# A two-block sequence model on one core: second FFN halves tile by tile, weight low parts on VectorE, folded transforms, two decay levels put by ScalarE

## The chip, the cores and the metric

The kernel runs on one core of one Trainium2 chip. The metric is the time of one execution on the device in microseconds (us), lower is better. TensorE (PE in the rows, PEld for its weight loads), VectorE (DVE), ScalarE (ACT), GpSimd (POOL) and the DMA queues of SyncE (SP) run side by side and meet at semaphores.

## The reference, cut to what matters

Two model blocks run one after the other on 512 tokens of width 1024 and on 256 context tokens; all arithmetic is float32.

```python
def half_ffn(h, shift, scale, gate, wg, wu, wd):
    return h + 0.5 * gate * swiglu(modulate(rms_norm(h), shift, scale), wg, wu, wd)
def swiglu(x, wg, wu, wd):
    return (jax.nn.silu(x @ wg) * (x @ wu)) @ wd
def step(s, inp):                       # hgrn2_chunk_scan; the GLA of block two has the same form
    ...
    scores = jnp.einsum('bhtsd,bhsd->bhts', qb[:, :, :, None, :] * decay, kb)
    o = scores @ vb + (qb * jnp.exp(cum)) @ s
    s_new = jnp.exp(last[:, :, 0, :])[..., None] * s + jnp.einsum('bhsd,bhse->bhde', kb * jnp.exp(last - cum), vb)
def fft_conv(u, kern):
    l = u.shape[1]
    uf = jnp.fft.rfft(u.astype(jnp.float32), n=2 * l, axis=1)
    kf = jnp.fft.rfft(kern, n=2 * l, axis=0)
    return jnp.fft.irfft(uf * kf[None], n=2 * l, axis=1)[:, :l]
def hyena(u3, kern, hy_bias):
    v, x1, x2 = jnp.split(u3, 3, axis=-1)
    z = v
    for o, gate in enumerate((x1, x2)):
        z = gate * (fft_conv(z, kern[:, o]).astype(z.dtype) + hy_bias[o] * z)
    return z
```

Block one is a half FFN, the mixers (HGRN2 with 4 heads of 128, and hyena), a projection and a second half FFN. Block two is two layers of GLA (4 heads of 64), window attention and a short convolution, a projection and an FFN.

## The kernel before, in words

**Layout.** Activations lie feature by token: `H` is [128, 8, 768], 512 latent tokens and 256 context tokens. A weight matrix is streamed as tiles of 128x1024 float32 (512 KB), 392 of them in one order (`in_stream`). Each product of a weight tile is made of three passes, `wr_hi` x `xx_hi`, `wr_hi` x `xx_lo`, `wr_lo` x `xx_hi`, on rounded high parts (type float32r) and their remainders. A tile has 8 steps (6 in the last third of an FFN's second half).

**The ring of weight tiles.** There are 2 buffers `raw` for the stream, 2 for the modulation rows (`in_mod_stream`), and 4 places of `wr_hi` and `wr_lo`. SP loads tile t once the low part of tile t-2 is made (L2324), and behind it in the same queue a modulation tile (L2330) once that buffer is used. ScalarE rounds (`split_tile`, L494) tile n+4 when PE is done with tile n. GpSimd subtracts (L2355, in a loop of its own over all tiles) and counts `tile_lo`, for which PE waits before it uses a tile and SP before it loads the next.

**FFN.** In three thirds of 8, 8 and 6 hidden tiles: `pe_ffn` takes gate and up tiles in turn. VectorE multiplies (L850 `ff_raw`), ScalarE rounds the hidden tile (L809), VectorE subtracts its low part (L856 `hid_lo`) and counts `hid_ready`. The second half of a third has 8 tiles. Two of them go as a pair (`pe_pair`, L438): with `lead` = F - 2 the first tile's F - 2 leading steps, then the second's, then the last steps in turn, so that both end together. The next two go one by one. VectorE adds each to `H` (`dve_residual`, L900) and thereby frees its PSUM slot; there are two. In block one and in block two's first FFN, VectorE makes the modulation vectors between (`dve_mod_tile`, L539): for each modulation tile one product over 128x1024 for each of 2 vectors (1 in some loops).

**HGRN and GLA units** (8 and 2 x 4, `pe_unit`, `act_unit`, `dve_unit`). For each of seven levels (block length 64, 32, ..., 1) VectorE makes exponents (L1078, L1079 `u_ex`), ScalarE takes exp (L1024), VectorE makes the two factors (L1106, L1107 `u_Z`), PE multiplies them (L983) and VectorE puts the result in the score matrix `u_P` under a mask (L1118). Before level 1, VectorE folds five chunks' states: `u_S` (L1142, L1144), in GLA, which has two heads in 128 partitions, each first through a mask `blk` (L1138). PE has steps of weight tiles between levels (L454).

**Hyena** (`pe_hyena`, `dve_hyena`). Four channel groups of two convolutions. Each is: 4 transposes (L1612), a copy (L1682 `hu`), the transform (L1621, 4 x 8 products with `dft`), products with the kernel's spectrum on VectorE (L1696 to L1711), the inverse (L1632, 8 products of 512 columns with `idft`), the gate (L1715, L1720). PE takes a weight tile (L410) behind the transform and another behind the inverse.

**Order.** Each engine's program is written out by hand; nothing reorders it.

## Time and profile before

| | |
|---|---|
| median of 3 runs | 3790.6 us (3789.75 to 3802.39) |
| profiled execution, its own time | 3798.3 us |
| span of the profiled execution | 3796.5 us |
| mean granted TensorE clock | 0.965 of full |
| PE, PEld busy | 92%, 75% |
| DVE, ACT, POOL busy | 53%, 30%, 26% |

The parts of the span, from the first matmuls of each norm: filters 0 to 159, block one's first FFN to 737, its mixers to 1424 (HGRN to 1110, hyena to 1326), its second FFN to 1831, block two's first mixers to 2394 (GLA to 2175), its first FFN to 2968, second mixers to 3410, second FFN to 3784. Matmuls are pipelined, so the time from one start to the next counts, rather than their duration: 0.23 us for 512 columns of float32r. A float32 matmul appears as two records.

### The profile page before, as it was taken

What the parts mean: (1) busy time and instruction counts of PE and PEld (TensorE: products, weight loads), DVE (VectorE), ACT (ScalarE), POOL (GpSimd) and SP (SyncE); (2) the same over time, 40 slices, a digit from 0 to 9 for tenths busy, and PEclk for the clock granted to TensorE, in tenths of its full rate; (3) what the DMA queues carried; (4) which work ended last, traced back from release to release, by engine and by line L of the source; (5) the groups of instructions that cost most, each with busy time, mean ns of one, the idle gap of its engine ahead of it and who ended that gap; (6) DMA issues with size and microseconds to landing.
All of it is one profiled execution on the core that took longest, in us unless ns stands there. A gap on an engine that the chain in (4) does not pass through costs nothing.

```text
span 3796.5 us, 50206 instructions
## 1 busy us (share of the span) xinstructions
PE 3503.6 (92%) x18584; PEld 2837.3 (75%) x18584; DVE 2010.7 (53%) x3025; ACT 1149.5 (30%) x1620; POOL 1003.3 (26%) x412
## 2 busy tenths in 40 slices
PE   6799999898889999999888889999999988989998
PEld 2388888787777777777677657788888767668887
DVE  5766341538844368783467575644331466762112
ACT  1221212344421123222433264321212332543222
POOL 2133223321121144444210101223223211123443
PEclk9899999999999999999989899999999988899999
DMA  5233332321132135453110101233322211112222
GB/s 197 94 125 129 123 111 78 132 67 34 40 107 64 52 116 174 172 174 107 62 67 23 56 17 34 99 111 133 122 103 66 77 40 34 45 44 84 94 94 94
DMA packets 101863, 341.46 MB, mean 90 GB/s; under 512 B 10159, under 2 KB 21551, under 8 KB 100240
## 3 DMA queue, kind: packets, MB, share of 16 engines
q1 hardware_dynamic: 82760, 301.90, 23.4%
q10 hardware_dynamic: 18952, 37.51, 2.8%
q8 instruction: 100, 1.64, 0.2%
q14 instruction: 51, 0.42, 0.0%
HBM read 325.21 MB, written 14.16 MB: 89 GB/s over the span
## 4 chain that ended last, share of the span: by engine, by line
issue 76%; POOL 19%; DMA 1%; PE 1%; DVE 1%; POOLq 0%; ACT 0%; ACTq 0%; SPq 0%; DVEq 0%
POOL wr_lo L2355 19%; PE ps L1259 1%; DMA raw<-in_stream 0%; DMA hyena_k<-fst 0%; PE ps L1266 0%; DVE mod_out L539 0%; DMA raw<-in_mod_stream 0%; PE ps L410 0%; POOLq L2354 0%; POOLq L2351 0%; DVE fnorm L1398 0%; ACTq L1319 0%; DVE H L740 0%; POOL wr_lo L2348 0%; PE ps L438 0%
## 5 line engine op out<-in xcount | busy, mean ns | idle before, releaser
L2355 POOL TENSOR_TENSOR wr_lo<-raw,wr_hi 128x1024 fp32r<-128x1024 f32 x388 | 970.0, 2504 | 2642.2 <-ACT wr_hi L494 2642.1
L410 PE MATMUL ps<-xx_hi,wr_hi 128*128 128x512 f32 x1728 | 689.1, 399 | 6.8 <-DVE H L900 5.7
L410 PE MATMUL ps<-xx_hi,wr_lo 128*128 128x512 f32 x1728 | 683.4, 395 | 0.0
L410 PE MATMUL ps<-xx_lo,wr_hi 128*128 128x512 f32 x1728 | 681.7, 395 | 0.0
L494 ACT ACTIVATE wr_hi<-raw 128x1024 fp32r<-128x1024 f32 x388 | 411.5, 1061 | 590.9 <-PE ps L410 309.0
L539 DVE CUSTOM_DVE_ANT_0 ps<-raw,cb 128x1024 f32<-128x1024 f32 x240 | 400.3, 1668 | 56.0 <-DMA raw<-in_mod_stream 25.8
L850 DVE TENSOR_TENSOR ff_raw<-ps,ff_gate 128x768 f32<-128x768 f32 (+1 forms) x88 | 72.6, 825 | 657.8 <-PE ps L410 650.3
L410 PEld LDWEIGHTS ps<-xx_hi,wr_hi 128*128 128x128 f32 x1728 | 326.6, 189 | 86.3 <-DVE H L900 6.5
L410 PEld LDWEIGHTS ps<-xx_lo,wr_hi 128*128 128x128 f32 x1728 | 326.6, 189 | 73.8 <-issue 2.1
L410 PEld LDWEIGHTS ps<-xx_hi,wr_lo 128*128 128x128 f32 x1728 | 326.3, 189 | 72.2
L900 DVE SCALAR_TENSOR_TENSOR H<-ps,hgv,H 128x512 f32 (+3 forms) x168 | 106.1, 659 | 285.5 <-PE ps L438 150.0
L809 ACT ACTIVATE hid_hi<-ff_raw 128x768 f32 (+1 forms) x88 | 65.1, 740 | 545.8 <-DVE ff_raw L850 545.7
L410 PE MATMUL ps<-xc_hi,wr_lo 128*128 128x256 f32 x816 | 230.2, 282 | 0.0
L410 PE MATMUL ps<-xc_lo,wr_hi 128*128 128x256 f32 x816 | 229.8, 282 | 0.0
L410 PE MATMUL ps<-xc_hi,wr_hi 128*128 128x256 f32 x816 | 228.8, 280 | 0.0
L410 PE MATMUL ps<-hid_hi,wr_hi 128*128 128x512 f32 (+1 forms) x528 | 163.4, 363 | 21.9 <-DVE H L900 21.7
L983 PEld LDWEIGHTS ps<-u_Z 64*128 64x128 f32 (+1 forms) x1568 | 129.1, 200 | 63.4 <-DVE u_Z L1107 49.4
L983 PE MATMUL ps<-u_Z 64*128 64x64 f32 (+1 forms) x1568 | 140.1, 287 | 34.7 <-DVE u_Z L1107 34.6
L438 PE MATMUL ps<-hid_hi,wr_hi 128*128 128x512 f32 (+1 forms) x528 | 159.5, 356 | 4.1 <-DVE H L900 2.2
L410 PE MATMUL ps<-hid_hi,wr_lo 128*128 128x512 f32 (+1 forms) x528 | 160.8, 359 | 0.0
L802 ACT ACTIVATE ff_gate<-ps 128x768 f32<-128x768 f32 (+1 forms) x88 | 62.1, 705 | 326.0 <-PE ps L410 318.1
L410 PE MATMUL ps<-hid_lo,wr_hi 128*128 128x512 f32 (+1 forms) x528 | 160.5, 358 | 0.0
(383 smaller groups left out, 6193.9 us busy)
## 6 DMA issues: line engine op xcount, KB each, us to landing
raw<-in_stream SPq DMA_DIRECT2D x392, 512.0 KB, 3.3
raw<-in_mod_stream SPq DMA_DIRECT2D x168, 512.0 KB, 4.3
hK<-hyena_k ACTq DMA_DIRECT2D x4, 1152.0 KB, 6.0
h_kept<-H ACTq DMA_DIRECT2D x2, 2048.0 KB, 9.0
hyena_k<-fst ACTq DMA_DIRECT2D x14, 256.0 KB, 11.2
H<-in_h ACTq DMA_DIRECT2D x1, 3072.0 KB, 15.5
h_kept<-H ACTq DMA_DIRECT2D x1, 3072.0 KB, 9.9
H<-h_kept ACTq DMA_DIRECT2D x1, 3072.0 KB, 9.8
```

The source lines that it names most:

```text
L410: last = pe.matmul(gslot(slot)[:, col:col + n], w, rhs[part], start=(bi == 0 and pi == 0), stop=(bi == len(blocks) - 1 and pi == 2))
L438: last = pe.matmul(gslot(slots[t])[:, col:col + n], w, rhs[part], start=(k == 0 and pi == 0), stop=(k == steps - 1 and pi == 2))
L494: act.activation(wr_hi[:, s, :], raw[:, s % RAW, :], ACT.Copy).then_inc(tile_hi, 1)
L539: ins = dve.tensor_tensor_reduce(out=product, in0=raw[:, RAW + place, :], in1=cb[:, v, :], scale=1.0, scalar=0.0, op0=ALU.mult, op1=ALU.ad ...
L802: act.activation(ff_gate[:, q, 0:n], gslot(slot)[:, 0:n], ACT.Silu).then_inc(slot_free[slot], 1)
L809: act.activation(hid[0][:, bass.ds(i * 2 + q, 1), 0:n], ff_raw[:, q:q + 1, 0:n], ACT.Copy).then_inc(hhi_ready, 1)
L850: dve.tensor_tensor(ff_raw[:, q, 0:n], gslot(slot)[:, 0:n], ff_gate[:, q, 0:n], ALU.mult).then_inc(slot_free[slot], 1)
L900: ins = dve.scalar_tensor_tensor(out=H[:, bass.ds(m, 1), a:b], in0=gslot(slot)[:, a:b].unsqueeze(1), scalar=hgv[:, bass.ds(m, 1), v], in1= ...
L983: last = pe.matmul(m[:, j * NX + c * HD:j * NX + (c + 1) * HD], Z[r, c * CH:(c + 1) * CH], queries[r, c * per:(c + 1) * per, 0 if bw else ...
L1259: last = pe.matmul(m[:, h * NX:(h + 1) * NX], fh[:, 1, h * NX + t * P:h * NX + (t + 1) * P], fw3[:, 2 * o + h, :], start=True, stop=True)
L2355: nc.gpsimd.tensor_tensor(wr_lo[:, s, :], raw[:, s % RAW, :], wr_hi[:, s, :], ALU.subtract).then_inc(tile_lo, 1)
```

## The change

- **Second FFN halves.** `pe_pair` loses `lead`; the eight tiles of a second half go one by one (`pe_tile`), the first with a wait for each hidden tile.
- **Low parts on VectorE.** A new function subtracts a tile's low part on VectorE; it is called in the FFNs, in block one's mixers and merge, and in block two's projections. GpSimd keeps the first four tiles and 20 in each of block two's mixers. So 348 of the 392 move.
- **Folded transforms.** A signal v is folded into v[t] + v[512-t] and v[t] - v[512-t] (`hfold`, 3 VectorE instructions). The transform takes 20 products of 128 columns for 32, the inverse 5 of 258 and 4 of 256 for 8 of 512. The even and odd halves are put together by four VectorE instructions in place of one.
- **Levels 64 and 32** of every unit are copied into `u_P` by ScalarE (one copy of half the partitions, and two of a quarter), with no mask. PE makes at level 64 only the half that is needed.
- **States per head.** In GLA each head's states are made apart (10 products of 64 columns for 5 of 128, stored 64 wide), and the mask product goes.

```diff
+        def dve_low_tile(dve, tally):
+            ahead = tally.n["tile_used"] - 1 + RING
+            if tally.i is None and ahead >= n_tiles:
+                return
+            s = tally.n.get("tile_hi", 0) % RING
+            dve.wait_ge(tile_hi, tally.next("tile_hi"))
+            dve.tensor_tensor(wr_lo[:, s, :], raw[:, s % RAW, :], wr_hi[:, s, :], ALU.subtract).then_inc(tile_lo, 1)
...
-                    pe_pair(pe, tally, F, lambda k: wide_spans(hid, k, with_ctx), (hid_ready, before), F - 2)
-                    for q in range(2):
-                        pe_tile(pe, tally, [[(k, wide_spans(hid, k, with_ctx)) for k in range(F)]])
+                    for q in range(4):
+                        pe_tile(pe, tally, [[(k, wide_spans(hid, k, with_ctx)) for k in range(F)]],
+                                (hid_ready, before) if q == 0 else None)
...
                         dve.wait_ge(slot_free[slot], tally.read("group"))
+                        dve_low_tile(dve, tally)
                         if vectors:
                             dve_mod_tile(dve, tally, 2 * q + 1, vectors, mslot(0))
...
                         dve.wait_ge(hid_ready, tally.next("hid_ready"))
+                        dve_low_tile(dve, tally)
...
             for c in order[:5]:
-                last = pe.matmul(m[:, c * P:(c + 1) * P], U["ktok"][:, c * P:(c + 1) * P], vt(c),
-                                 start=True, stop=True)
+                for j in range(nsub):
+                    f = slice(j * P // nsub, (j + 1) * P // nsub)
+                    last = pe.matmul(m[f, c * P:c * P + P // nsub], U["ktok"][:, c * P + f.start:c * P + f.stop],
+                                     vt(c)[:, f], start=True, stop=True)
...
+                at_level.append((tally.take("misc_done"), tally.now("misc_done"), tally.read("misc_done")))
+                if li - 2 in BLOCK_LEVELS:
+                    act_put(act, tally, U, li - 2, nsub, toks, *at_level[li - 2])
                 ahead(li)
...
+            for n in range(HD // b):
+                keys = slice((2 * n + bw) * b, (2 * n + bw + 1) * b)
+                queries = (2 * n + 1 - bw) * b
+                ins = act.activation(dst, src, ACT.Copy)
...
             for u in range(8):
                 def ahead(li, nxt=u + 1):
+                    if (nxt == 8 and li == 2) or (nxt < 8 and li == 4) or li == 5:
+                        dve_low_tile(dve, tally)
+                    if nxt == 8 and li == 1:
+                        dve_low_tile(dve, tally)
...
             def gates_ready():
                 skip_tiles(tally, 4)
+                for _ in range(4):
+                    dve_low_tile(dve, tally)
...
-                    for c in range(NFREQ):
-                        for t in range(4):
-                            last = pe.matmul(m[:, c * P:(c + 1) * P], dft[:, t, c * P:(c + 1) * P], hu[:, t, :],
+                    for i, (c, t) in enumerate(DFT_STEPS):
+                        last = pe.matmul(m[:, c * P:(c + 1) * P], dft[:, i, :], hu[:, t, :],
...
+            for at in MIX2_FIRST:
+                pool.wait_ge(tile_lo, at + RING)
+                with pool.Fori(at // RING + 1, (at + MIX2_TILES) // RING + 1) as i:
```

Where the instructions stand. On PE in hyena, the first convolution (the 24 matmuls of a weight tile, L410 before and L413 now, stand between the transform and its inverse). Before:

```order
L1612 MATMUL ps<-ident,hv_118 128x128 x4
L1621 MATMUL ps<-hu,dft 128x128 x32
...
L1632 MATMUL ps<-idft,hY 128x512 x8
```

Now:

```order
L1665 MATMUL ps<-ident,hfold 128x128 x4
L1674 MATMUL ps<-hu,dft 128x128 x20
...
L1687 MATMUL ps<-idft,hY 128x258 x5
L1687 MATMUL ps<-idft,hY 128x256 x4
```

Both transforms are shorter, and nothing is moved past them.

On VectorE in the loop of gate and up tiles of block one's second FFN, with two vectors; `tile_used` is PE's mark on a tile. Before:

```order
L850 TENSOR_TENSOR ff_raw<-ps,ff_gate 128x512 [waits tile_used]
L539 ISA ps,modacc<-raw,cb 128x1024 [waits mod_landed1,slot_free1]
...
L539 ISA ps,modacc<-raw,cb 128x1024 [waits dve_step]
...
L856 TENSOR_TENSOR hid_lo<-ff_raw,hid_hi 128x512
...
L539 ISA ps,modacc<-raw,cb 128x1024 [waits mod_landed0]
```

Now:

```order
L860 TENSOR_TENSOR ff_raw<-ps,ff_gate 128x512 [waits tile_used]
...
L505 TENSOR_TENSOR wr_lo<-raw,wr_hi 128x1024 [waits tile_hi]
L549 ISA ps,modacc<-raw,cb 128x1024 [waits mod_landed1]
...
L549 ISA ps,modacc<-raw,cb 128x1024 [waits dve_step]
...
L867 TENSOR_TENSOR hid_lo<-ff_raw,hid_hi 128x512
...
L505 TENSOR_TENSOR wr_lo<-raw,wr_hi 128x1024 [waits tile_hi]
L549 ISA ps,modacc<-raw,cb 128x1024 [waits mod_landed0]
```

A subtraction stands behind `ff_raw` and another behind `hid_lo`, each ahead of the next modulation tile.

On VectorE in a GLA unit of the first layer, from the state updates to level 2. Before:

```order
L1138 TENSOR_TENSOR u_Z<-ps,blk 128x128 [waits dve_step]
L1144 SCALAR_TENSOR_TENSOR u_S<-u_S,dec,u_Z 128x128 [waits dve_step]
L1106 TENSOR_TENSOR u_Z<-u_ex_154,gk 128x12x32 [waits ex_out,misc_free1]
L1107 TENSOR_TENSOR u_Z<-u_ex_154,gq 128x12x32
L1078 TENSOR_TENSOR u_ex_153<-u_cum 128x48x8
L1079 TENSOR_TENSOR u_ex_153<-u_cum 128x48x8
L1118 COPY_PREDICATED u_P<-masks,ps 128x12x64 [waits misc_done]
L1106 TENSOR_TENSOR u_Z<-u_ex_155,gk 128x24x16 [waits ex_out,misc_free0]
```

Now:

```order
L1182 SCALAR_TENSOR_TENSOR u_S<-u_S,dec,ps 128x64 [waits dve_step] x4
L1144 TENSOR_TENSOR u_Z<-u_ex_155,gk 128x12x32 [waits ex_out,misc_free1]
L1145 TENSOR_TENSOR u_Z<-u_ex_155,gq 128x12x32
L1116 TENSOR_TENSOR u_ex_154<-u_cum 128x48x8 [waits z_ready]
L1117 TENSOR_TENSOR u_ex_154<-u_cum 128x48x8
L1144 TENSOR_TENSOR u_Z<-u_ex_156,gk 128x24x16 [waits ex_out,misc_done]
```

The five mask products and the masked copy of level 64 are gone from VectorE's row; the wait for PE's level (`misc_done`) stays.

## Rows read from the trace of the kernel before

**Rows 1.** Page (a group: busy us, mean ns); windows: engines' busy us (instructions), clock, DMA.

```profile
PE 3503.6 (92%) x18584; PEld 2837.3 (75%) x18584; DVE 2010.7 (53%) x3025; ACT 1149.5 (30%) x1620; POOL 1003.3 (26%) x412
...
L539 DVE CUSTOM_DVE_ANT_0 ps<-raw,cb 128x1024 f32<-128x1024 f32 x240 | 400.3, 1668 | 56.0 <-DMA raw<-in_mod_stream 25.8
...
850.00:1058.00 208.00, 184.83 (x1166) 158.43 (x1165) 184.48 (x340) 96.45 (x125) 36.03 (x16) 1.00 0.12 39
1110.00:1326.00 216.00, 205.18 (x1047) 157.37 (x1048) 94.48 (x132) 29.25 (x36) 35.22 (x15) 0.98 0.20 59
1424.00:1831.00 407.00, 376.63 (x1591) 302.82 (x1589) 287.75 (x306) 125.20 (x151) 182.56 (x68) 0.97 0.45 152
1925.00:2175.00 250.00, 216.41 (x1692) 183.91 (x1691) 173.35 (x258) 74.54 (x89) 31.21 (x13) 0.90 0.09 29
3060.00:3240.00 180.00, 159.00 (x1085) 126.98 (x1086) 129.37 (x233) 56.84 (x80) 24.19 (x10) 0.85 0.11 36
3410.00:3784.00 374.00, 366.89 (x1593) 299.80 (x1592) 71.94 (x95) 114.62 (x132) 156.51 (x65) 0.99 0.27 90
```

**Rows 2.** Timeline, one convolution of hyena: start us, us, engine, line, what.

```profile
1169.77 0.69 DVE L1682 COPY hu<-ps 128x512 f32<-128x512 f32 x1 [2.41 <-PE ps L1612]
1169.95 1.06 ACT L494 ACTIVATE wr_hi<-raw 128x1024 fp32r<-128x1024 f32 x1
1170.51 7.41 PE L1621 MATMUL ps<-hu,dft 128*128 128x128 f32 x64 [0.85 <-DVE hu L1682]
...
1176.17 0.75 DVE L1671 SCALAR_TENSOR_TENSOR hv<-hyp,vecs,hv 128x511 f32<-128x511 f32 x1
1178.06 0.69 DVE L1696 TENSOR_TENSOR hY<-ps,hK 128x512 f32<-128x512 f32 x1 [1.14 <-PE ps L1621]
...
1182.54 0.29 DVE L1711 TENSOR_TENSOR hY<-hY,hK 128x128 f32<-128x128 f32 x1
...
1183.22 7.03 PE L1632 MATMUL ps<-idft,hY 128*128 128x512 f32 x16
```

**Rows 3.** One line's instructions over the whole trace: count, ns min/median/max.

```profile
L539 DVE DVE_READ_ACCUMULATOR2_ANT modacc<- x272: 76/140/144, 64.0 to 2811.4; 128x1 f32 x136
L539 DVE CUSTOM_DVE_ANT_0 ps<-raw,cb x240: 1232/1234/3414, 188.6 to 2808.8; 128x1024 f32<-128x1024 f32 x120
L856 DVE TENSOR_TENSOR hid_lo<-ff_raw,hid_hi x88: 691/958/2753, 197.7 to 3751.7; 128x768 f32 x44, 128x512 f32 x44
L1078 DVE TENSOR_TENSOR u_ex<-u_cum x112: 410/421/2615, 827.8 to 3196.9; 128x256 f32<-128x256 f32 x84, 128x384 f32<-128x384 f32 x28
L2355 POOL TENSOR_TENSOR wr_lo<-raw,wr_hi x388: 2338/2397/3460, 192.8 to 3768.4; 128x1024 fp32r<-128x1024 f32 x194
```

**Rows 4.** Timeline, block one's second FFN, end of a first half and a pair.

```profile
1530.66 2.70 POOL L2355 TENSOR_TENSOR wr_lo<-raw,wr_hi 128x1024 fp32r<-128x1024 f32 x1 [5.51 <-ACT wr_hi L494]
...
1531.43 2.47 DVE L856 TENSOR_TENSOR hid_lo<-ff_raw,hid_hi 128x512 f32 x1 [0.26 <-DVE modacc L539]
...
1535.36 0.39 PE L438 MATMUL ps<-hid_hi,wr_lo 128*128 128x512 f32 x1
1538.62 0.50 PE L410 MATMUL ps<-hid_hi,wr_hi 128*128 128x512 f32 x1 [2.87 <-DVE H L900]
```

**Rows 5.** Waits (total us, times, longest), whole trace, then 1424 to 1831 alone.

```profile
PE ps L410 <- DVE H L900: 27.4, 31, 3.0
...
PE ps L410 <- DVE H L900: 19.5, 11, 3.0
```

**Rows 6.** DMA issues: size, median us from issue to landing.

```profile
raw<-in_mod_stream SPq DMA_DIRECT2D x168, 512.0 KB, 4.3
```

**Rows 7.** Timeline, VectorE in a GLA unit of the first layer.

```profile
1941.95 0.28 DVE L1138 TENSOR_TENSOR u_Z<-ps,blk 128x128 f32<-128x128 f32 x1
...
1945.39 0.56 DVE L1106 TENSOR_TENSOR u_Z<-u_ex,gk 128x384 f32<-128x384 f32 x1
...
1947.27 1.02 DVE L1118 COPY_PREDICATED u_P<-masks,ps 128x768 f32<-128x768 uint8 x1
```

More of the change, by code:

```diff
@@ L9 @@
+import itertools
 from contextlib import ExitStack
@@ L37 @@
 LEVELS = (64, 32, 16, 8, 4, 2, 1)
+BLOCK_LEVELS = (0, 1)
 RING = 4
@@ L414, in pe_tile, with pe_pair @@
             tally.passed("tile_used")
-        def pe_pair(pe, tally, steps, spans, order, lead=0):
+        def pe_pair(pe, tally, steps, spans, order):
             s = tile_slot(tally)
@@ L425, in pe_pair @@
                 frees.append(tally.free("group", 1))
-            turns = [(t, k) for t in range(2) for k in range(lead)]
-            turns += [(t, k) for k in range(lead, steps) for t in range(2)]
-            for t, k in turns:
+            for k, t in itertools.product(range(steps), range(2)):
                 if k == 0:
@@ L1113, in put @@
                 dve.wait_ge(misc_done, tally.now("misc_done"))
+                if li in BLOCK_LEVELS:
+                    return
+                if li - 1 in BLOCK_LEVELS:
+                    dve.wait_ge(misc_free[tally.place("misc_done", 2)], tally.read("misc_done", 2))
                 dst = U["P"].rearrange("p j (c n h b) -> p j c n h b", c=nch, h=2, b=b)[:, :, :, :, 0 if bw else 1, :]
@@ L1592, in dve_hgrn @@
                          ahead, head if u < 7 else None)
+            for _ in range(2):
+                dve_low_tile(dve, tally)
             def gates_ready():
                 skip_tiles(tally, 4)
+                for _ in range(4):
+                    dve_low_tile(dve, tally)
                 for back in (1, 2):
@@ L1630, in pe_hyena @@
                     m = mslot(place)
-                    for c in range(NFREQ):
-                        last = pe.matmul(m[:, 0:NX], hY[:, c, :], idft[:, c, :], start=(c == 0),
-                                         stop=(c == NFREQ - 1))
+                    for i, (c, odd) in enumerate(IDFT_STEPS):
+                        n = 256 if odd else 258
+                        last = pe.matmul(m[:, NX * odd:NX * odd + n], hY[:, c, :], idft[:, i, 0:n],
+                                         start=(i in (0, IDFT_EVEN)), stop=(i in (IDFT_EVEN - 1, len(IDFT_STEPS) - 1)))
                     last.then_inc(misc_done, 1)
@@ L1673, in conv, with fold @@
                 dve.wait_ge(done[0], tally.next(done[1]))
-            conv(0, 0, (hv_ready, "hv_ready"))
+            def fold(src):
+                dve.tensor_tensor(hfold[:, 0, 1:256], src[:, 1:256], src[:, 511:256:-1], ALU.add).then_inc(hv_ready, 1)
+                dve.tensor_tensor(hfold[:, 1, 1:256], src[:, 1:256], src[:, 511:256:-1], ALU.subtract
+                    ).then_inc(hv_ready, 1)
+                dve.tensor_copy(hfold[:, :, 0], src[:, 256::-256]).then_inc(hv_ready, 1)
+                tally.passed("hv_ready", 3)
+            conv(0, 0, (dve_step, "dve_step"))
+            fold(hvs[0][:, 0, :])
             for g in range(4):
@@ L1718, in dve_hyena @@
-                    dve.wait_ge(misc_free[ms], tally.read("misc_done"))
-                    dve.wait_ge(misc_free[tally.place("misc_done", 1)], tally.read("misc_done"))
-                    dve.tensor_tensor(hv[:, 0, :], hv[:, 0, :], hv[:, 1 + o, :], ALU.mult
-                        ).then_inc(z_done if o else hv_ready, 1)
-                    dve.wait_ge(z_done if o else hv_ready, tally.next("z_done" if o else "hv_ready"))
-                    if not o:
-                        dve.wait_ge(hv_ready, tally.now("hv_ready"))
+                    v, even, odd = hv[:, 0, :], mslot(ms)[:, 0:257], mslot(ms)[:, NX:NX + 256]
@@ new lines, in dve_hyena @@
+                    dve.scalar_tensor_tensor(out=v[:, 0:257], in0=v[:, 0:257], scalar=vec("hy_bias", 4 * o + g),
+                                             in1=even, op0=ALU.mult, op1=ALU.add).then_inc(dve_step, 1)
+                    dve.scalar_tensor_tensor(out=v[:, 511:256:-1], in0=v[:, 511:256:-1],
+                                             scalar=vec("hy_bias", 4 * o + g), in1=even[:, 1:256],
+                                             op0=ALU.mult, op1=ALU.add).then_inc(dve_step, 1)
@@ new lines, in dve_hyena @@
+                    dve.wait_ge(dve_step, tally.next("dve_step", 2))
+                    dve.tensor_tensor(v[:, 0:256], v[:, 0:256], odd, ALU.add).then_inc(dve_step, 1)
+                    dve.tensor_tensor(v[:, 511:256:-1], v[:, 511:256:-1], odd[:, 1:256], ALU.subtract
+                        ).then_inc(misc_free[ms], 1)
+                    dve.wait_ge(dve_step, tally.next("dve_step"))
+                    dve.wait_ge(misc_free[ms], tally.read("misc_done"))
+                    if o:
+                        dve.tensor_tensor(v, v, hv[:, 2, :], ALU.mult).then_inc(z_done, 1)
+                        dve.wait_ge(z_done, tally.next("z_done"))
+                    else:
+                        dve.tensor_tensor(v, v, hv[:, 1, :], ALU.mult).then_inc(dve_step, 1)
+                        dve.wait_ge(dve_step, tally.next("dve_step"))
+                        fold(v)
@@ L2591, in _tables @@
     inv[:, 512] = S[:, 0]
-    t["idft"] = (inv.T / 1024.0).reshape(8, P, NX).transpose(1, 0, 2).astype(np.float32).copy()
+    inv = inv.T / 1024.0
+    steps = []
+    for c, b in DFT_STEPS:
+        full = np.concatenate([C, S], 1)[:, c * P:(c + 1) * P]
+        w = full[b % 2 * P:(b % 2 + 1) * P].copy()
+        even = b < 2
+        if b % 2 == 0:
+            w[0] = full[256 if even else 0]
+        if c == 4:
+            w[:, 1 if even else 0:None if even else 1] = 0.0
+            if b == 2:
+                w[0, 0] = 1.0
+        if c < 2 and not even:
+            w[:] = 0.0
+            w[0] = 1.0
+        steps.append(w)
+    t["dft_fold"] = np.stack(steps, 1).astype(np.float32)
+    steps = np.zeros((P, len(IDFT_STEPS), 258), np.float32)
+    for i, (c, odd) in enumerate(IDFT_STEPS):
+        w = inv[c * P:(c + 1) * P, 0:256 if odd else 257].copy()
+        if c == 4:
+            w[0 if odd else 1:1 if odd else None] = 0.0
+        steps[:, i, 0:w.shape[1]] = w
+    t["idft_fold"] = steps
     tok = np.arange(NX)
```

89 lines of the change are left out of this document (60 added, 29 removed).

## The prediction

> **What bounds the kernel now.** I read the engine totals and the stretches first [rows 1]: PE is busy for 92% of the span, VectorE for 53%, GpSimd for 26%. So a saving counts where it takes work off PE or ends one of PE's waits. The stretches differ. In block two's last FFN (3410 to 3784) PE takes 1593 matmuls in 374 us, 0.235 us each, and VectorE has 72 us of work: nothing but PE counts there. In block one's second FFN (1424 to 1831) the same number of matmuls (1591) takes 407 us, with VectorE at 288 us: 33 us go to waits. In HGRN's units (850 to 1058) VectorE and PE are both busy for 184 of 208 us, so they pace each other. In GLA (1925 to 2175, 3060 to 3240) both wait, and the granted clock is 0.90 and 0.85. Then the durations of single lines [rows 3]. A VectorE operation with two SBUF inputs has a floor and a maximum some 2 us above it: 1.23 and 3.41 us for L539, 0.69 and 2.75 for L856, 0.41 and 2.62 for L1078. The difference is about one GpSimd subtraction, 2.4 us. In the timeline [rows 4] `hid_lo` of 512 columns takes 2.47 us from 1531.43, and a GpSimd subtraction runs from 1530.66 to 1533.36: it is blocked until that ends. How much is it? L539 loses 240 x (1.668 - 1.234) = 104 us over the trace [rows 1]. In block one's second FFN the floors give 48 modulation tiles x 2.75 (two of L539 and two reads) = 132, 44 x 0.69 = 30 for `ff_raw` and `hid_lo`, and by my estimate 45 for residuals, sums, the norm and small ones: 207 of 288 us, so some 80 are blocking there, and for the whole trace I reckon with 300.
>
> The Trainium skill ("SBUF — State Buffer", section "SBUF: two separate sides") says that VectorE and GpSimd take a shared port pair as an exclusive lock, and a VectorE operation with two SBUF inputs blocks against GpSimd. The trace agrees, by the numbers above.
>
> **Part 1, folded transforms.** 32 products of 128 columns take 7.15 us (64 records in 7.41 us with the last one's tail), 0.223 us each; 8 products of 512 columns take 6.86 us of 7.03 [rows 2], 0.86 each. Per column this is 1.74 ns and 1.68 ns, so 256 columns lie between the two forms: 0.43 us. Removed: 12 x 0.223 = 2.68 us in the transform, and 6.86 - 9 x 0.43 = 2.99 us in the inverse. Eight convolutions: 8 x 5.67 = 45.3 us, all on PE, in a stretch where PE is busy for 205 of 216 us. What did the removed time cover? VectorE's products with the spectrum run from 1178.06 to 1182.83, 4.8 us, behind the transform and beside a weight tile of 24 x 0.23 = 5.5 us. Before them stand now, behind the copy `hu` (end 1170.46): a subtraction of 1.23 us that starts when ScalarE's rounding is done (1171.01), and in a group's first convolution two short convolutions, 4.3 us at their floors. That ends at 1176.6. The transform ends at 1170.5 + 4.5 = 1175.0. So VectorE is 1.5 us late, of which the tile's 5.5 against 4.8 us absorb 0.6: PE waits about 1 us, in three of the eight (the first group has no subtraction there, the second convolutions have less work). The four put-together operations and the fold, some 3.7 us in place of 1.4, lie beside the second tile of 5.5 us. Before the first convolution the fold is open, 1 us. Sum: -45 + 3 + 1 = **-41 us**. Bounds: -45 if VectorE is never late, and -17 if a product of 256 columns costs what one of 512 does, so that the inverse gives nothing.
>
> **Part 2, low parts on VectorE.** A subtraction over 128x1024 with two SBUF inputs is not in the trace on VectorE; L539 with that form has 1.23 us, and L856 0.69 at 512 columns and 0.96 at 768, which leads to 1.22 [rows 3]. 348 x 1.23 = 428 us on VectorE, against some 300 us of blocking less what stays in the stretches where GpSimd goes on. What stands behind each subtraction on VectorE's queue is in the order rows: in the FFN the next modulation tile and `hid_lo`.
>
> Block one's second FFN: of a pair of tiles (11.0 us on PE) VectorE has 4 x 1.37 us (L539 with its read of 0.14 [rows 3]), 2 x 0.69, and now 2 x 1.23: 9.3 us, no longer blocked. Before, it was 6.9 us and one or two blockings of 2 us. A weight tile's low part must be there three tiles (16 us) after its rounding, and it comes within 7 us. A modulation tile is issued behind a subtraction and lands in 4.3 us [rows 6]; until VectorE wants it there pass 2.75 + 0.69 + 1.23 = 4.7 us. That just holds. So PE's waits there should go, save the chain of sums over the last eight tiles (about 9 us; it has a subtraction more and a blocking less), and a new one: the first down tile now reaches its last step after 7/8 x 5.5 = 4.8 us, and the last `hid_lo` is ready after 0.69 + 1.23 + 2.75 + 0.69 + waits = 5.6 us, twice. 33 - 9 - 2 = **-22 us**, bounds 0 and -33.
>
> HGRN: per unit of 29.5 us VectorE gets 2 or 3 subtractions (2.5 us), loses about 5 us of blocking (L1078 at 2.6 us for 0.42 is the sample) and two masked copies (1.02 us at 768 columns [rows 7], so some 0.4 at 256). Both engines pace each other, the subtractions stand at levels 4 and 5, where VectorE is behind already. I take -0.75 us per unit, -6, and +2 where four subtractions stand ahead of the head norm's gates: **-4 us**, bounds -16 and +10.
>
> **Part 3, no lead in the second halves.** After a pair both slots are full, and PE waits for the residual: 27.4 us over the trace, 19.5 of them in block one's second FFN [rows 5], counted above. The gap at 1535.36 [rows 4] is one, and the clock is at half behind it. The other three FFNs: 27.4 - 19.5 = **-8 us**. The wait for `hid_lo` that the pair covered is 4.8 us away in block two's last FFN, without modulation tiles, against 2.9 us of chain, and 7.4 against 6.2 us where context tokens make a tile 8.4 us long: nothing new.
>
> **Part 4, puts on ScalarE and states per head in GLA.** From 1941.95 to 1945.39 VectorE takes 3.4 us for the masks and states [rows 7]; five operations of 64 columns are about 1.5 us: -1.9. Two masked copies of 1.02 us (some 0.7 at the second layer's 512 columns) go. That is 4 us per unit in the first layer and 3.3 in the second, 29 us over 8 units, in the half of a unit in which VectorE runs without a pause and PE waits for its factors. PE pays 5 more small products per unit, 0 to 1 us. ScalarE pays for them: its rounding copy over 1024 columns takes 1.06 us [rows 2], and each of the three copies covers 768 or fewer, on an engine busy for 75 of 250 us [rows 1]. I take three quarters: **-22 us**, bounds 0 and -45; the upper one has the clock too, which lies at 1.2 GHz for a tenth to a seventh of these stretches and should return with fewer waits.
>
> The Trainium skill ("ScalarE: Activation LUTs", section "Rules for kernel authors") says to do such simple operations on VectorE, not ScalarE. By rows, a ScalarE copy of 1024 columns takes 1.06 us [rows 2] and a VectorE operation of that size 1.23 [rows 3]. Were each copy dearer by half, ScalarE would still have two thirds of these stretches free, and the sum stays.
>
> **Sum.** -41 - 22 - 4 - 8 - 22 = -97 us from the profiled execution's 3798.3. It lies 8 us over the median of 3790.6, which I take as the base: **3694 us**.
>
> **Rivals.**
> - *More comes back* (22%). HGRN -16, GLA -40, block one's FFN -30, hyena -43, the rest -10: -139, 3652 us. For it: the clock of 0.85 to 0.90. Against: PE's own work in GLA grows.
> - *Only PE's saving stays* (12%). VectorE's queue is as full in HGRN and in the FFN as before: -41 in hyena, -8, +10 in HGRN, 0 and 0 elsewhere: 3752 us. For it: 428 us come and 300 go.
> - *The excess is not GpSimd's* (5%). If VectorE's slow operations had another cause (the landing DMA), the subtractions add 68 x 1.23 = 84 us to 288 of 407 us in block one's second FFN, and that comes to 372 us with every wait on top, about +15 there and +15 in HGRN: 3790 - 41 - 8 - 15 + 30 = 3756 us.
> - *Slower* (5%). Modulation tiles arrive late. If SP issues one only behind the subtraction directly ahead of its use, a tile costs 4.3 + 2.75 + 0.69 + 1.23 = 9.0 us in place of 5.5, over 48 tiles with two vectors: +168, and the 22 us are not gained: 3694 + 190 = 3884 us. It decides where the landing takes longer than the 4.7 us above. Against it: two buffers stand between, and SP waits for the subtraction of two tiles before.
> - *The change doesn't do what it says* (2%), the inverse at full price: 3694 + 24 = 3718 us.
>
> **How the numbers follow.** The forecast has 54%. The range reaches over the rivals at 3752 and below, down to where most of the first rival lies: 3645 to 3756. It leaves out the slow one and the tails. A measurement of this kernel tells about 0.5% (19 us) from no change: faster by more than that 0.92, within it 0.03, slower 0.05.
>
> **What would show it.** Hyena should last near 175 us for 216, with transforms of 4.5 and 3.9 us for 7.15 and 6.86. L539 at 1.23 us nearly everywhere outside block two's mixers. Block one's second FFN near 385 us, with no 3 us gap at the start of down tiles. VectorE busy for about 2,120 us. GLA's units some 3 us shorter, the clock there above 0.9. It would be wrong if PE waits in the FFN for VectorE's subtraction or SP's modulation tiles come late, or if hyena's tile no longer covers VectorE.

## The result, and the profile after

The changed kernel takes 3743.9 us (median of 4 runs) against 3795.9 us for the kernel before beside it: ratio 0.987, 95% interval 0.984 to 0.991. That is 52 us less, where 97 were forecast. Its profiled execution has a span of 3741.4 us against 3796.5, 55 less.

The page's totals, and two of VectorE's groups (line, engine, operation, tiles, shape, count | busy us, mean ns | idle before, releaser):

```profile
PE 3491.2 (93%) x18488; PEld 2826.7 (76%) x18488; DVE 2072.1 (55%) x3349; ACT 1169.8 (31%) x1668; POOL 129.6 (3%) x64
...
L505 DVE TENSOR_TENSOR wr_lo<-raw,wr_hi 128x1024 fp32r<-128x1024 f32 x348 | 426.2, 1225 | 100.5 <-ACT wr_hi L495 69.0
...
L549 DVE CUSTOM_DVE_ANT_0 ps<-raw,cb 128x1024 f32<-128x1024 f32 x240 | 295.3, 1231 | 51.4 <-DMA raw<-in_mod_stream 36.4
```

L549 is the modulation product that stood at 1668 ns [rows 1]: it is at its floor of 1232 ns [rows 3]. A low part takes 1.225 us (taken: 1.23). VectorE took on 426 us of work and is busy for 61 us more (2072 us, where about 2120 were forecast).

Now the stretches, each engine's busy us (instructions), then PE's granted clock, the DMA share and GB/s: HGRN, hyena, block one's second FFN, GLA of both layers, the last FFN, and 17 us in one GLA unit:

```profile
816.00:1050.00 234.00, 216.58 (x1367) 188.08 (x1368) 187.47 (x383) 122.05 (x173) 0.00 (x0) 0.99 0.14 44
1088.00:1261.00 173.00, 164.22 (x881) 141.27 (x882) 108.82 (x186) 28.62 (x35) 0.00 (x0) 0.98 0.24 70
1359.00:1740.00 381.00, 366.61 (x1591) 299.49 (x1592) 279.86 (x378) 125.86 (x153) 0.00 (x0) 0.99 0.47 162
1837.00:2056.00 219.00, 199.75 (x1444) 153.75 (x1444) 134.92 (x202) 62.88 (x79) 19.08 (x8) 0.79 0.07 22
2903.00:3163.00 260.00, 230.67 (x1400) 172.33 (x1400) 136.10 (x244) 89.47 (x125) 38.29 (x16) 0.85 0.14 44
3362.00:3731.00 369.00, 364.02 (x1589) 299.69 (x1588) 142.41 (x160) 113.59 (x131) 0.00 (x0) 0.99 0.28 90
1879.00:1896.00 17.00, 16.64 (x70) 10.42 (x72) 2.13 (x3) 2.26 (x3) 2.35 (x1) 0.55 0.10 31
```

Hyena went from 214 to 173 us, block one's second FFN from 407 to 380 [rows 1]. The last row is the surprise: PE is busy for 16.64 of 17 us, in 70 records, at a clock of 0.55. Over the stretches from the norm to GLA's end, the granted clock is 0.84 and 0.85, where it was 0.91 and 0.88 before: it fell, where it should have risen.

The length of each stage, from the starts of its first products, in us (one profiled execution each, read to about 1 us; the last five columns are experiments, below):

| stage | before | after | g1 grouped | g3 whole states | g6 lead | g7 GpSimd lows | h1 folds only |
|---|---|---|---|---|---|---|---|
| block one, first FFN | 579 | 563 | 574 | 573 | 571 | 573 | 572 |
| HGRN units | 246 | 234 | 235 | 234 | 237 | 243 | 246 |
| hyena | 214 | 173 | 172 | 173 | 173 | 173 | 174 |
| block one, second FFN | 408 | 380 | 380 | 380 | 385 | 388 | 409 |
| block two, first norm to GLA's end | 288 | 317 | 277 | 292 | 278 | 275 | 284 |
| block two, first FFN | 574 | 572 | 571 | 561 | 569 | 561 | 570 |
| its second norm to GLA's end | 245 | 260 | 233 | 239 | 233 | 234 | 244 |
| last FFN | 373 | 369 | 369 | 368 | 373 | 369 | 373 |

GLA became 44 us longer (29 and 15), where 22 less were forecast. The timeline shows where (start us, duration us, engine, line, operation): the output products of a unit of the first layer, L1019 for the values and L1022 for the states, then the same in the layer's last unit.

```profile
1932.32 0.66 PE L1019 MATMUL ps<-u_P,vtok 128*64 128x128 f32 x2 [2.11 <-DVE u_P L1160]
1932.91 0.69 PE L1022 MATMUL ps<-u_lf,u_S 64*64 64x128 f32 x2
1933.53 0.69 PE L1019 MATMUL ps<-u_P,vtok 128*64 128x128 f32 x2
...
2046.07 0.43 PE L1022 MATMUL ps<-u_lf,u_S 64*64 64x128 f32 x2
2046.43 0.43 PE L1019 MATMUL ps<-u_P,vtok 128*64 128x128 f32 x2
2046.79 0.43 PE L1022 MATMUL ps<-u_lf,u_S 64*64 64x128 f32 x2
```

Two records are one float32 product. "64*64 64x128" is a weight tile 64 rows deep and 64 columns wide, "128*64 128x128" one 128 deep. From one turn of depth to the next there pass 0.61 us, and 0.36 us in the last unit, where the clock is full. A whole block of this layer has 44 records; it takes 11.8 to 13.0 us in the first three units and 7.66 us in the last. In the kernel before, with all products 128 deep, the same 44 records took 2.65 to 4.14 us. Two of its rows, in the layer's last unit:

```profile
2117.03 0.44 PE L1000 MATMUL ps<-u_P,vtok 128*64 128x128 f32 x4
2117.25 0.44 PE L1003 MATMUL ps<-u_lf,u_S 128*64 128x128 f32 x4
```

Both kernels are written in the same order: value and state product of one head, then of the other. Yet the rows of before show four value records, then four state records, a new four every 0.22 us. The products of the two heads, which fill different halves of the columns, run side by side there; their single records start 0.01 to 0.06 us apart. In the changed kernel two records stand alone between the turns.

### The profile page after: what moved, and what is told of

Same layout as the page of the kernel before. It is cut to its first block, busy times and chain, and to the rows that moved or that the text cites. A ratio compares the mean times of both kernels' runs of the same rounds, so it can differ in the third digit from the quotient of the medians.

```text
span 3741.4 us, 49724 instructions
## 1 busy us (share of the span) xinstructions
PE 3491.2 (93%) x18488; PEld 2826.7 (76%) x18488; DVE 2072.1 (55%) x3349; ACT 1169.8 (31%) x1668; POOL 129.6 (3%) x64
## 4 chain that ended last, share of the span: by engine, by line
PE 79%; DVE 13%; ACT 3%; DMA 2%; issue 2%; ACTq 0%; POOL 0%; DVEq 0%; SPq 0%
PE ps L413 59%; PE ps L455 4%; PE ps L1001 2%; PE ps L439 2%; PE ps L2174 2%; PE ps L1019 1%; PE ps L1022 1%; PE ps L974 1%; DVE u_P L1160 1%; PE ps L2160 1%; PE ps L2146 1%; PE ps L1687 1%; DMA raw<-in_mod_stream 1%; PE ps L1674 1%; PE ps L2149 1%
## 5 line engine op out<-in xcount | busy, mean ns | idle before, releaser
L413 PE MATMUL ps<-xx_hi,wr_hi 128*128 128x512 f32 x1728 | 683.5, 396 | 0.5 <-ACT ff_gate L812 0.4
L413 PE MATMUL ps<-xx_hi,wr_lo 128*128 128x512 f32 x1728 | 680.5, 394 | 0.0
L413 PE MATMUL ps<-xx_lo,wr_hi 128*128 128x512 f32 x1728 | 678.2, 393 | 0.0
L505 DVE TENSOR_TENSOR wr_lo<-raw,wr_hi 128x1024 fp32r<-128x1024 f32 x348 | 426.2, 1225 | 100.5 <-ACT wr_hi L495 69.0
L413 PEld LDWEIGHTS ps<-xx_hi,wr_hi 128*128 128x128 f32 x1728 | 325.4, 188 | 75.7 <-issue 2.9
L413 PEld LDWEIGHTS ps<-xx_lo,wr_hi 128*128 128x128 f32 x1728 | 325.5, 188 | 71.4 <-issue 0.2
L413 PEld LDWEIGHTS ps<-xx_hi,wr_lo 128*128 128x128 f32 x1728 | 325.5, 188 | 71.1
L549 DVE CUSTOM_DVE_ANT_0 ps<-raw,cb 128x1024 f32<-128x1024 f32 x240 | 295.3, 1231 | 51.4 <-DMA raw<-in_mod_stream 36.4
L413 PE MATMUL ps<-hid_hi,wr_hi 128*128 128x512 f32 (+1 forms) x1056 | 317.8, 355 | 4.1 <-DVE hid_lo L867 2.1
L413 PE MATMUL ps<-hid_hi,wr_lo 128*128 128x512 f32 (+1 forms) x1056 | 319.1, 356 | 0.0
L413 PE MATMUL ps<-hid_lo,wr_hi 128*128 128x512 f32 (+1 forms) x1056 | 317.2, 354 | 0.0
L413 PE MATMUL ps<-xc_hi,wr_lo 128*128 128x256 f32 x816 | 229.8, 282 | 0.0
L413 PE MATMUL ps<-xc_lo,wr_hi 128*128 128x256 f32 x816 | 229.3, 281 | 0.0
L413 PE MATMUL ps<-xc_hi,wr_hi 128*128 128x256 f32 x816 | 227.9, 279 | 0.0
L413 PEld LDWEIGHTS ps<-hid_hi,wr_hi 128*128 128x128 f32 x1056 | 174.4, 188 | 36.6 <-DVE hid_lo L867 2.9
L2440 POOL TENSOR_TENSOR wr_lo<-raw,wr_hi 128x1024 fp32r<-128x1024 f32 x40 | 96.1, 2404 | 2944.8 <-ACT wr_hi L495 2944.8
L413 PEld LDWEIGHTS ps<-hid_hi,wr_lo 128*128 128x128 f32 x1056 | 173.8, 188 | 28.4
L413 PEld LDWEIGHTS ps<-hid_lo,wr_hi 128*128 128x128 f32 x1056 | 173.2, 188 | 29.0
```

Source lines behind the costliest of these rows:

```text
L413: last = pe.matmul(gslot(slot)[:, col:col + n], w, rhs[part], start=(bi == 0 and pi == 0), stop=(bi == len(blocks) - 1 and pi == 2))
L505: dve.tensor_tensor(wr_lo[:, s, :], raw[:, s % RAW, :], wr_hi[:, s, :], ALU.subtract).then_inc(tile_lo, 1)
L549: ins = dve.tensor_tensor_reduce(out=product, in0=raw[:, RAW + place, :], in1=cb[:, v, :], scale=1.0, scalar=0.0, op0=ALU.mult, op1=ALU.ad ...
L2440: nc.gpsimd.tensor_tensor(wr_lo[:, s, :], raw[:, s % RAW, :], wr_hi[:, s, :], ALU.subtract).then_inc(tile_lo, 1)
```

## The experiments

**Theory A:** a change between products of 128 and of 64 rows holds TensorE up, and the clock falls behind it. **B:** products of 64 rows are slow in themselves. **C:** the clock fell for another reason and is all of it. None of the three has the lost overlap of the two heads; g2 tells it apart. The first four separate them and test the copies on ScalarE. The kernel before took 3789.6 us beside them.

**g1, one change of depth per unit.** The start flag is now set once per PSUM bank and head (`c % 4 == 0`), and no longer with every value product. No run tries the flags by themselves, but p2, below, has them in this form and is slow all the same.

```
+for of_states in (False, True):
     for c in range(nch):
         for j in range(nsub):
+            if not of_states:
-            last = pe.matmul(m[f, cc], vt(c)[:, f], U["P"][:, j, cc], start=True, ...)
+                last = pe.matmul(m[f, cc], vt(c)[:, f], U["P"][:, j, cc], start=c % 4 == 0, ...)
-            if at_order > 0:
+            elif at_order > 0:
                 last = pe.matmul(m[f, cc], U["S"][f, at_order, 0:P // nsub], U["eq"][f, cc], ...)
```

> The changed kernel, with the output products of a unit in another order: first all products of the values (128 rows deep), then all products of the states (64 rows deep), so that the depth of the product changes once per unit and not 16 to 20 times; the same numbers are computed. Theory A (each change between a 128-row and a 64-row product holds TensorE up, and the clock falls behind it): the output block of a unit takes about 3 us for 11.8, eight units give back 8 x 8 = 65 us, 3744 - 65 = 3680 us. Theory B (the 64-row products are slow whatever stands beside them): the block stays near 11.8 us, 3744 us. Theory C (only the clock, which fell for another reason, is to blame): 3744 us within 10, with the clock at half in the block.

Measured: 3672.7 us, ratio 0.968 (0.966 to 0.970), 71 us less than the changed kernel. The timeline of the last unit of the first layer:

```profile
2015.44 1.53 PE L1021 MATMUL ps<-u_P,vtok 128*64 128x128 f32 x24
2016.90 1.31 PE L1024 MATMUL ps<-u_lf,u_S 64*64 64x128 f32 x20
```

The same 44 records in 2.77 us for 7.66. In the 20 short records the two heads' row halves alternate, and they run side by side again: a pair of records starts every 0.109 us, as the pairs of 128-row products ahead of them. So neither short products nor going from one 64-row tile to the other costs anything. Theory B falls. C falls as well: the clock was 1.00 in both blocks, and what was changed is the order with its flags. GLA's stages are 277 and 233 us, and the granted clock over them is 0.91 and 0.92 again, for 0.84 and 0.85. So the low clock came with the order too.

**g2, a chunk's products in pairs.**

```
+for of_states in (False, True):      # inside the loop over chunks
     for j in range(nsub):
```

> The changed kernel, with the products of a chunk's two heads put in pairs: both value products, then both state products, so that the depth changes 8 to 10 times in a unit's output block and not 16 to 20 times. Theory A (each change costs a fixed time): about half the loss comes back, the block takes about 7 us, 3744 - 33 = 3711 us. Theory B and theory C: 3744 us as it was.

Measured: 3706.4 us, ratio 0.976 (0.972 to 0.980). The last unit's timeline:

```profile
2035.28 0.44 PE L1021 MATMUL ps<-u_P,vtok 128*64 128x128 f32 x4
2035.65 0.44 PE L1024 MATMUL ps<-u_lf,u_S 64*64 64x128 f32 x4
```

Four records between changes, and still 0.37 us from one change to the next, as with two (0.36). Record by record, the four are the products of two heads side by side (starts 0.01 us apart), the two are the product of one head alone. In both cases two passes run one behind the other. Unhindered these take 2 x 0.109 = 0.22 us, as in g1, so a change adds 0.15 us. The blocks agree: g2 has 10 changes and g1 has one, and 9 x 0.15 = 1.35 us is what lies between 4.12 and 2.77. The changed kernel has 20 changes, 19 x 0.14 = 2.7 us over g1. The other 2.2 of its 4.9 us are the lost overlap: 21 groups stand one behind the other where 11 did, 10 x 0.22. So the changed kernel paid twice, and g2 gives one payment back whole and half of the other.

**g3, states per head undone.**

```
-for j in range(nsub):
-    last = pe.matmul(m[f, c * P:c * P + P // nsub], U["ktok"][...], vt(c)[:, f], ...)
+last = pe.matmul(m[:, c * P:(c + 1) * P], U["ktok"][:, c * P:(c + 1) * P], vt(c), ...)
...
-    last = pe.matmul(m[f, cc], U["S"][f, at_order, 0:P // nsub], U["eq"][f, cc], ...)
+    last = pe.matmul(m[f, cc], U["S"][:, at_order, f], U["eq"][:, cc], ...)
```

> The changed kernel with the states per head undone: key-value products 128 columns wide, the mask of the two heads and 128-wide states on VectorE again, state products 128 rows deep. Theories A and B: the output block is back at about 2.5 us (-8 x 8.5 = -68), VectorE has its 1.9 us per unit again (+15): 3744 - 53 = 3691 us. Theory C: VectorE's 15 us alone count, 3759 us.

Measured: 3689.6 us, ratio 0.973 (0.970 to 0.977): 54 us less than the changed kernel and some 17 more than g1. VectorE's state work in g3, ten operations of which four stand here, then in g1, all five:

```profile
1947.37 0.28 DVE L1178 TENSOR_TENSOR u_Z<-ps,blk 128x128 f32<-128x128 f32 x1
1947.69 0.23 DVE L1182 COPY u_S<-u_Z 128x128 f32<-128x128 f32 x1
1947.95 0.29 DVE L1178 TENSOR_TENSOR u_Z<-ps,blk 128x128 f32<-128x128 f32 x1
1948.28 0.35 DVE L1184 SCALAR_TENSOR_TENSOR u_S<-u_S,dec,u_Z 128x128 f32<-128x128 f32 x1
```

```profile
1936.15 0.22 DVE L1182 COPY u_S<-ps 128x64 f32<-128x64 f32 x1
1936.41 1.23 DVE L1184 SCALAR_TENSOR_TENSOR u_S<-u_S,dec,ps 128x64 f32<-128x64 f32 x4
```

1.5 us for 3.4, as forecast. The states per head are worth 17 us, once the order of their products is right; in the changed kernel they cost 54.

**g4, no copies on ScalarE.** `BLOCK_LEVELS = (0, 1)` becomes `()`.

> The changed kernel with the first two levels' masked copies on VectorE again in every unit, states per head kept. If the copies on ScalarE save what the prediction reckoned (two copies of about 1 us in GLA's units, 0.4 in HGRN's, at three quarters), it takes 8 x 1.3 + 8 x 0.6 = 15 us longer: 3759 us. If ScalarE's copies only take the place of VectorE's in the chain, 3744 us within 5. If ScalarE's copies are themselves late for the next level, it is shorter, 3735 us. Theories A to C expect the same long output block in it.

Measured: 3743.8 us, ratio 0.987 (0.984 to 0.989), the changed kernel's time: the second of the three cases. No gain or cost of the copies shows there.

The next four build on g1, or on the kernel before, which took 3783.5 us beside them, 6 us less than beside g1. So what they differ from g1 by is given twice: from the medians, and from the ratios to the kernel before.

**g5, g1 with `BLOCK_LEVELS = ()`.**

> The kernel with the output products in two groups (3672.7 us), with the first two levels' masked copies on VectorE again. They were worth nothing while the output block was 11.8 us long. If that was because the long block hid them, they now show 10 to 15 us: 3685 us. If ScalarE's copies stand in the same chain as VectorE's did, it stays at 3673 us within 5.

Measured: 3675.3 us, ratio 0.972 (0.969 to 0.975), 3 us more than g1 by the medians and 14 by the ratios, while the profiled execution took 3660. Its interval overlaps that of g1. The pair was measured again as j1 and j2, below.

**g6, g1 with the pair and its lead in the second FFN halves.**

```
-for q in range(4):
-    pe_tile(pe, tally, [[...]], (hid_ready, before) if q == 0 else None)
+pe_pair(pe, tally, F, ..., (hid_ready, before), F - 2)
+for q in range(2):
+    pe_tile(pe, tally, [[...]])
```

> The kernel with the output products in two groups (3672.7 us), with the second FFN halves begun by a pair of tiles as before the change. The prediction gave the loss of the pair 8 us in three FFNs, and in block one's second FFN a part of 22 us. If the stage lengths are read rightly (-14.6, -1.6, -4.0 us in the three, and 3 us twice in block one's second), it takes 10 to 25 us longer: 3683 to 3698 us. Rival: VectorE's low parts alone took those waits away, and the pair costs nothing without GpSimd beside it: 3673 us within 5.

Measured: 3694.1 us, ratio 0.976 (0.973 to 0.979), 21 us more than g1 by the medians and 31 by the ratios. The two profiled executions are only 8 us apart, and the stages show these: 5 us in block one's second FFN and 4 in the last FFN. Where the rest of the medians' difference lies, the traces don't show. PE's wait for the residual (total us, times, longest) in g6 and, after it, in the changed kernel:

```profile
PE ps L413 <- DVE H L917: 9.5, 26, 0.9
```

```profile
PE ps L413 <- DVE H L915: 2.0, 4, 0.6
```

Before, that wait had 27.4 us [rows 5]. Without GpSimd beside VectorE the pair costs a third of that; with GpSimd and without the pair (g7) it is gone from the list of waits, and the first down tiles wait 10.5 us in all for `hid_lo`, for 1.9 in g1.

**g7, g1 with all low parts on GpSimd.** The calls of `dve_low_tile` do nothing, and GpSimd's loop runs over all tiles again.

> The kernel with the output products in two groups (3672.7 us), with all low parts on GpSimd again. The prediction's terms for the low parts (block one's second FFN -22 with the pair's share, HGRN -4) give +20 to +26, so 3693 to 3699 us. Had all that the stages show beside the transforms come from them (block one's FFNs 14.6 + 28.2, HGRN 13), it is +56: 3729 us. If VectorE's operations are slow for another reason than GpSimd, nothing or less: 3670 us and VectorE's modulation products still at 1.67 us.

Measured: 3688.0 us, ratio 0.974 (0.971 to 0.978), 15 us more than g1 by the medians and 23 by the ratios: 8 in HGRN and 8 in block one's second FFN by the stages. The modulation products in g7:

```profile
L549 DVE CUSTOM_DVE_ANT_0 ps<-raw,cb 128x1024 f32<-128x1024 f32 x240 | 388.4, 1618 | 50.1 <-DMA raw<-in_mod_stream 19.7 <-DVE mods L561 13.5 <-ACT cb L534 5.0
```

1618 ns for 1231, with nothing changed but the engine of the subtractions: the excess was GpSimd's. In block one's second FFN either edit alone brings most of the 28 us (pair undone 20, low parts moved 23): they don't add up, and both shorten the wait for the residual.

**h1, the kernel before with the folded transforms alone.**

> The kernel before with the folded transforms alone. The prediction's term is -41 us (8 convolutions of 5.67 us less 4 for VectorE late), against 3789.6 us: 3748 us, bounds -45 and -17. Blocked by GpSimd, VectorE's fold and put-together operations have less room than in the changed kernel: if that counts, it is -35, 3755 us.

Measured: 3749.9 us, ratio 0.991 (0.988 to 0.995), 34 us less, where 41 were expected; its hyena lasts 174 us for 214, so 40 by the stage.

**p1 and p2, is it the depth alone?** In HGRN all products are 128 columns wide, and no second head runs beside them. Rival D is that it takes the 64-column halves too. For this measurement its state products are cut to 64 rows, which leaves out half of the states' contribution. p1 has the values first, p2 has them in turn:

```
-last = pe.matmul(m[f, cc], U["S"][f, at_order, 0:P // nsub], U["eq"][f, cc], ...)
+r = f if nsub == 2 else slice(0, HD)
+last = pe.matmul(m[f, cc], U["S"][r, at_order, 0:P // nsub], U["eq"][r, cc], ...)
```

> A measurement, not a candidate: the grouped kernel without the copies on ScalarE, in which HGRN's output leaves out half of the states' contribution (its state products are 64 rows deep for 128), so its values differ. HGRN runs at the full clock and has one value and one state product of 128 columns for each chunk. Grouped, all four value products stand before the four short state products: one change of depth. Theories A, B and C: the block of 16 records stays at 2.0 us, as with 128 rows (theory B, short products are slow: above 2.5 us).

> The same measurement, half of HGRN's state contribution left out, with value and state products of a chunk in turn: seven changes of depth per unit and not one. By GLA's last units at the full clock a change costs (7.66 - 2.77)/18 = 0.27 us there, in pairs (4.12 - 2.77)/8 = 0.17 us. Theory A (it is the change of depth): 2.0 + 6 x 0.17 to 0.27 = 3.0 to 3.6 us for the block at the full clock. Rival D (it needs 64-column halves of the array as in GLA, or the change of the column half with it): 2.0 us as in the grouped measurement.

The first unit's output block in p1, then two of its eight pieces in p2, and a later unit of p2:

```profile
849.70 1.13 PE L1021 MATMUL ps<-u_P,vtok 128*128 128x128 f32 x8 [0.70 <-DVE u_P L1163]
850.76 1.16 PE L1025 MATMUL ps<-u_eq,u_S 64*128 64x128 f32 x8
```

```profile
839.17 0.49 PE L1028 MATMUL ps<-u_eq,u_S 64*128 64x128 f32 x2
839.59 0.49 PE L1024 MATMUL ps<-u_P,vtok 128*128 128x128 f32 x2
...
898.40 0.49 PE L1024 MATMUL ps<-u_P,vtok 128*128 128x128 f32 x2
898.82 0.77 PE L1028 MATMUL ps<-u_eq,u_S 64*128 64x128 f32 x2
899.52 0.79 PE L1024 MATMUL ps<-u_P,vtok 128*128 128x128 f32 x2
```

In p1 a product's two records take 0.22 us, and the block 2.21 (forecast 2.0; with all products 128 deep it is 2.02). In p2 0.42 us pass from change to change, and the block is 3.37 us, in a stretch at the full clock (2.4 GHz). So a change adds 0.19 us: once in p1 (2.21 - 2.02), and six times more in p2 (3.37 - 2.21 = 1.16). Rival D falls: the depth alone does it. The expectation of 0.27 us for a change was too high, since it laid the lost overlap on the changes too. From 898.82 it is 0.70 to 0.73 us from change to change: the clock went to 1.2 GHz in the middle of the block, and PE had worked without a wait since the block began at 897.59. p2's HGRN lasts 253 us for p1's 238, 15 us for 48 changes more, 0.31 each. That is more than 0.19, as the granted clock was below 0.9 in four of p2's eight output blocks, and in one of p1's. The whole of p2 took 3671.0 us and that of p1 3682.0, one execution each: two FFNs without any edit between them were 11 and 9 us shorter in p2 (see the last section).

**j1 and j2, g1 and g5 again, with more executions.**

> The changed kernel with grouped output products again, with more rounds, beside the next one. It had 0.968 of the time before. If puts on ScalarE are worth what the prediction said, it is 10 to 15 us faster than the next one; if they are worth nothing, they agree within 5 us.

> The grouped kernel with the first two levels' copies on VectorE, with more rounds. It had 0.9716 in its median of four and a profiled execution of 3657.9 us, which contradict each other. By the stages of its trace (GLA 273 + 232 us against 277 + 233) ScalarE's copies cost 5 us: 3668 us, ratio 0.967. If they help: 3685 us.

Measured: 3674.5 us, ratio 0.969 (0.966 to 0.971), and 3683.1 us, ratio 0.971 (0.969 to 0.973). The intervals overlap. The copies' gain is 9 us here; it was 3 or 14 in the first pair. GLA's stages last 275 and 233 us in j1, 276 and 235 in j2. A unit of GLA's first layer (36.8 us long in both), windows of j1 and then j2:

```profile
1973.60:2010.40 36.80, 29.22 (x269) 24.89 (x268) 32.99 (x54) 7.88 (x10) 2.65 (x1) 0.91 0.10 30
```

```profile
1978.30:2015.10 36.80, 29.05 (x276) 24.89 (x274) 34.02 (x56) 6.10 (x7) 3.17 (x1) 0.91 0.10 30
```

VectorE is busy for 1 us less in j1, PE and the unit's length are as in j2. So the copies on ScalarE are worth something between nothing and 14 us, and GLA's stages show 3 of it. What takes VectorE's time in their place wasn't settled.

The fastest kernel is g1, the change with grouped output products: 3672.7 and 3674.5 us in its two measurements, 3.1 to 3.2% under the kernel before.

## Why the prediction was right and wrong

*Part 1, transforms, -41:* right, and so are its steps; PE waits for `hY` three times, 2.3 us in all, where the sum had 3. One convolution of the changed kernel, PE's transform and inverse:

```profile
1177.13 4.73 PE L1674 MATMUL ps<-hu,dft 128*128 128x128 f32 x40 [0.85 <-DVE hu L1746]
...
1187.99 4.17 PE L1687 MATMUL ps<-idft,hY 128*128 128x258 f32 x18 [0.65 <-DVE hY L1778]
1191.82 0.59 PE L413 MATMUL ps<-xx_hi,wr_hi 128*128 128x512 f32 x1
```

From 1177.13 to the next tile's start at 1181.62 are 4.49 us (forecast 4.5), from 1187.99 to 1191.82 3.83 (3.9). A product of 256 columns thus costs half of one of 512. Stage: -41 in the changed kernel, -40 alone. The bound of -17 was set wrong: nine products of 256 columns at the price of one of 512 are dearer than the eight before, so it should have been -10.

*Part 2, block one's second FFN, -22, bounds 0 and -33:* -28, for the reason given (L549 at its floor; the residual wait in this stage from 19.5 to 2.0 us, and all of PE's waits in it from 29 to 13). The granted clock rose from 0.97 to 0.99 as well, which the sum didn't have. The slower rival had no ground: VectorE waited for modulation tiles 18 times there, 8.1 us in all and never over 0.8. *HGRN, -4, bounds -16 and +10:* the stage is 12 shorter, 8 of it from the low parts (g7 243 us, g1 235). The blocking lost was worth more than the sum took; the other 4 us stay open. *Part 3, the three other FFNs, -8:* -4 in the last. In the other two nothing can be told: their lengths are 563 to 579 and 561 to 574 us over the seven kernels of the table, without regard to the pair.

*Part 4, GLA, -22, bounds 0 and -45:* +44. This is the whole miss. The step that failed is "PE pays 5 more small products per unit, 0 to 1 us". I counted how many products there are and not in which order they stand. The five more key-value products were indeed free (20 records in 1.33 us, for 10 in 1.35). But the state products had become 64 rows deep and stood in turn with the 128-row value products, head by head. That costs a toll at each change, and it takes away the overlap of the two heads. In the first layer it adds 7.66 - 2.77 = 4.9 us per unit at the full clock and 8 to 10 in the units where the clock had fallen, in the second 3.7 and 6. Over the eight output blocks this is 54 us. GLA's two stages are 67 us longer than in g1, since the clock was lower around the blocks too, and the whole kernel is 71. The sum had at most 8. With it taken out, GLA is at 277 and 233 us, 23 less than before: the forecast's -22, though most of it from the states (21 us of the stages, g3 less g1) and little from the copies, to which I had given half. The Trainium skill's row that the prediction cites on ScalarE ("ScalarE: Activation LUTs", section "Rules for kernel authors") names relu, max, min, add and mul, and no copy, so the copies' small worth is no test of it. "The clock there above 0.9" failed by the same cause: it was 0.84 and 0.85, and 0.91 and 0.92 in g1. The prediction also misread the clock before: a mean of 0.90 and 0.85 is a fifth and three tenths of the time at 1.2 GHz, not a tenth to a seventh.

The Trainium skill had the rule. "TensorEngine Tiling (Array Packing)", section "Key Properties", says that changing the tiling mode, as against only the tile, drains TensorE. It gives no price. The runs agree on both halves: the change of depth costs (0.15 us in GLA, 0.19 in HGRN), going between the two 64-row tiles in g1 does not. I had weighed pages on VectorE's port and on ScalarE, and passed over the engine that bounds the kernel. The trace of before didn't show a change's price in these blocks, but it showed the overlap that was at stake: 44 records in 2.65 us, four at a time. One head's product after the other, 22 products of 0.22 us are 4.8 us, 2.2 more per unit.

*Range and sum:* the time lies inside 3645 to 3756, by luck: the bounds were set for other rivals, and none had the cost in GLA. By stages the parts give -41 - 28 - 12 - 4 + 44 = -41; the profiled execution shows -55. Most of the difference is block one's first FFN, 16 us shorter (579 to 563), which no edit explains: g1 with the same code there has 574, h1 with the code of before 572.

## What to carry to other kernels

Where matmuls of unlike depth feed one result, write all of one depth first and then all of the other (in g1 with the start flag once per PSUM bank and head). If that can't be done, at least keep products that fill different column halves next to each other, as g2 does. Cutting a product to the rows that hold data saved nothing on PE here. It made a turn of one product cost 0.36 us, for 0.11 before, where its neighbours were deeper. When PE bounds the kernel, look at the order and shape of its products, not only at their number, before work is shifted to it from an engine that waits.
